# Residual stream by tokens: the second FFN products and the output projection move 512 weight columns past stationary activations

## What is computed

```python
for l in range(DEPTH):
    x = x + 0.5 * _swiglu(_rms_norm(x, ffn1_norm[l]), ffn1_w_gate[l], ffn1_w_up[l], ffn1_w_down[l])
    p = _rms_norm(x, mix_norm[l]) @ w_in[l]
    y_mla = _mla(p[..., :MLA_IN], ...)      # latent attention
    y_rwkv = _rwkv7(p[..., MLA_IN:], ...)   # recurrent mixing, in chunks of 64 tokens
    y = jnp.concatenate([_rms_norm(y_mla, out_norm_mla[l]), _rms_norm(y_rwkv, out_norm_rwkv[l])], axis=-1)
    x = x + y @ w_out[l]
    x = x + 0.5 * _swiglu(_rms_norm(x, ffn2_norm[l]), ffn2_w_gate[l], ffn2_w_up[l], ffn2_w_down[l])

def _swiglu(h, w_gate, w_up, w_down):       # 1024 -> 2816 -> 1024
    return (jax.nn.silu(h @ w_gate) * (h @ w_up)) @ w_down
```

## Time and profile before

| | |
|---|---|
| three runs | 1330.39, 1335.17, 1336.95 us (median 1335.17) |
| profiled execution, its own time | 1329.74 us |
| its span in the profile | 1328.0 us |
| mean granted TensorE clock | 0.976 of full |
| busy share of the span | TensorE 94%, weight loads 89%, VectorE 66%, ScalarE 39%, GpSimd 2% |
| read from memory | 172.57 MB, 131 GB/s over the span |

### The profile page before, as it was taken

One profiled execution on the slowest core, in us unless ns is written; L12 is line 12 of the kernel. 1 busy time (PEld: TensorE's weight loads), 2 busy tenths in 40 slices (PEclk: granted clock), 3 DMA queues, 4 the chain that ended last, 5 costly groups with the idle time before them and its releaser, 6 DMA issues.

```text
span 1328.0 us, 30142 instructions
## 1 busy us (share of the span) xinstructions
PE 1252.1 (94%) x12242; PEld 1181.2 (89%) x12242; DVE 871.3 (66%) x1498; ACT 515.8 (39%) x767; POOL 26.5 (2%) x26
## 2 busy tenths in 40 slices
PE   7999999997989999999989999999789998999998
PEld 6999999976876889999989999989668677999998
DVE  4666666687774866666666666666868558666665
ACT  3444444642121344444434444445322214344442
POOL 0000000020000000000000000000200000000000
PEclk8999999998999999999989999989999899999999
DMA  5666665531010335666546666646210103556563
GB/s 156 186 187 176 188 177 145 154 93 48 4 33 18 112 112 177 186 180 183 164 122 183 182 182 181 191 110 165 69 37 3 49 17 96 159 178 185 181 183 111
DMA packets 243396, 174.69 MB, mean 132 GB/s; under 512 B 10274, under 2 KB 228540, under 8 KB 243324
## 3 DMA queue, kind: packets, MB, share of 16 engines
q1 hardware_dynamic: 243324, 173.64, 44.6%
HBM read 172.57 MB, written 1.05 MB: 131 GB/s over the span
## 4 chain that ended last, share of the span: by engine, by line
PE 78%; DVE 16%; issue 2%; ACT 2%; DMA 2%; SPq 0%; DVEq 0%; ACTq 0%
PE bank L1247 21%; PE bank L1249 20%; PE bank L1248 20%; PE bank L1260 7%; DVE wlo L708 3%; PE bank L1271 2%; PE bank L1296 2%; ACT whi L530 1%; DVE xlo L738 1%; PE bank L1254 1%; DVE work L1072 1%; DVE root L724 1%; DVE root L725 1%; DVE work L942 1%; DMA raw<-in_ffn_w_up_dram 1%
## 5 line engine op out<-in xcount | busy, mean ns | idle before, releaser
L708 DVE TENSOR_TENSOR wlo<-raw,whi 128x1024 fp32r<-128x1024 f32 x324 | 394.8, 1221 | 261.4 <-ACT whi L530 260.5
L1247 PE MATMUL bank<-xhi,whi 128*128 128x256 f32 x1840 | 531.7, 289 | 18.7 <-DVE xlo L738 14.5
L1248 PE MATMUL bank<-xlo,whi 128*128 128x256 f32 x1840 | 524.7, 285 | 0.0
L1249 PE MATMUL bank<-xhi,wlo 128*128 128x256 f32 x1840 | 524.5, 285 | 0.0
L530 ACT ACTIVATE whi<-raw 128x1024 fp32r<-128x1024 f32 x324 | 338.7, 1049 | 307.2 <-PE bank L1249 266.3
L1247 PEld LDWEIGHTS bank<-xhi,whi 128*128 128x128 f32 x1840 | 357.7, 194 | 25.7 <-issue 11.9
L1248 PEld LDWEIGHTS bank<-xlo,whi 128*128 128x128 f32 x1840 | 357.8, 194 | 0.1
L1249 PEld LDWEIGHTS bank<-xhi,wlo 128*128 128x128 f32 x1840 | 357.3, 194 | 0.0
L1247 PE MATMUL bank<-hhi,whi 128*128 128x256 f32 x704 | 199.9, 284 | 0.8 <-DVE hlo L830 0.8
L1248 PE MATMUL bank<-hlo,whi 128*128 128x256 f32 x704 | 199.2, 283 | 0.0
L1249 PE MATMUL bank<-hhi,wlo 128*128 128x256 f32 x704 | 199.2, 283 | 0.0
(11 more groups left out here) (213 smaller groups left out, 1061.6 us busy)
## 6 DMA issues: line engine op xcount, KB each, us to landing
raw<-in_ffn_w_gate_dram SPq DMA_DIRECT2D x88, 512.0 KB, 3.9
raw<-in_ffn_w_up_dram SPq DMA_DIRECT2D x88, 512.0 KB, 3.8
raw<-in_ffn_w_down_dram SPq DMA_DIRECT2D x88, 512.0 KB, 3.5
raw<-in_w_in_dram SPq DMA_DIRECT2D x34, 512.0 KB, 4.0
raw<-in_w_out_dram SPq DMA_DIRECT2D x16, 512.0 KB, 3.3
raw<-in_w_in_dram SPq DMA_DIRECT2D x8, 256.0 KB, 3.3
raw<-in_w_q_up_dram SPq DMA_DIRECT2D x4, 384.0 KB, 3.7
work<-in_x_dram SPq DMA_DIRECT2D x1, 1024.0 KB, 6.6
```

The source lines that it names most:

```text
L708: V_.tensor_tensor(wlo[:, b.slot, 0:width], raw[:, b.slot, 0:width], whi[:, b.slot, 0:width].bitcast(F32), ALU.subtract).then_inc(lo_ready, 1)
L1247: mm(out, hi, mhi, start=start, stop=False, **kw)
L1248: mm(out, hi, mlo, start=False, stop=False, **kw)
L1249: return mm(out, lo, mhi, start=False, stop=stop, **kw)
```

## The change

x stays by tokens (the tile xtok: 128 tokens on the partitions, two of those, 1024 features along the free axis).

- The down products and the output projection swap the operands: 128 tokens of the activations are stationary, and 512 columns of the weights move. A block takes 12 matmuls of 512 columns, where it took 24 of 256. The first one of a bank starts the sum, so no bank is cleared.
- At each norm x is transposed in PSUM (turn_x, 16 transposes), after the residual is added; xhi and xlo are made from those banks. keep_clock is gone there.
- The squares are summed along the free axis by ScalarE itself (accum_out), in two instructions of 128x1024; TensorE's squares are gone.
- The row factors of the two halves of the output projection are applied by VectorE per token, in the residual (one instruction a quarter). GpSimd's additions, R's copy after rmsb and the step yn are gone.
- VectorE's splits of the second weight block (up 0, and r0 of the input projection) move from before the residual to behind the last xlo. ScalarE splits the third block before it squares.
- x is loaded and stored in four DMAs of 256 KB, without the transposes at both ends.

```diff
         def x_quarter(i):
-            return xT[:, 2 * i:2 * i + 2, :].rearrange("p t n -> p (t n)")
+            return xtok[:, i % 2, 512 * (i // 2):512 * (i // 2 + 1)]
...
-            def norm(st, phase, gain):
+            def norm(st, phase, gain, between):
                 for i in range(4):
-                    act.wait_ge(x_ready, quarter(phase, i))
+                    act.wait_ge(x_turned, turned(phase, i))
                     for t in (2 * i, 2 * i + 1):
-                        ins = nc.scalar.activation(xhi[:, t, :], xT[:, t, :], ACT.Copy, scale=col(gain, t))
+                        ins = nc.scalar.activation(xhi[:, t, :], turn_bank(phase, t), ACT.Copy, scale=col(gain, t))
                     ins.then_inc(st.sem, st.step(f"hi{i}"))
-                for i in range(4):
-                    nc.scalar.activation(xsq[:, 2 * i:2 * i + 2, :], xT[:, 2 * i:2 * i + 2, :],
-                                         ACT.Square).then_inc(st.sem, st.step(f"sq{i}"))
+                between()
+                if phase:
+                    act.wait_ge(x_ready, quarter(phase, 3))
+                for tt in range(2):
+                    ins = nc.scalar.activation(xsq[:, tt, :], xtok[:, tt, :], ACT.Square,
+                                               accum_out=stat[:, 192 + tt:193 + tt])
+                ins.then_inc(st.sem, st.step("sq"))
...
-                dve.wait_ge(stp.sem, stp.at(rnd, "ss"))
-                V_.tensor_scalar(root[:, 0, 0:2], bank[b0][:, 0:2], 1.0 / D, EPS, ALU.mult,
+                dve.wait_ge(sta.sem, sta.at(rnd, "sq"))
+                V_.tensor_scalar(root[:, 0, 0:2], stat[:, 192:194], 1.0 / D, EPS, ALU.mult,
                                  ALU.add).then_inc(st.sem, st.step("ms"))
...
-                    part = parts[:, 512 * i:512 * (i + 1)]
-                    V_.tensor_tensor(part.rearrange("p (t n) -> p t n", t=2),
...
-                        V_.tensor_tensor(x_quarter(i), x_quarter(i), part, ALU.add).then_inc(x_ready, 1)
+                    V_.scalar_tensor_tensor(x_quarter(i), bank[4 + i][:], root[:, 1, i % 2:i % 2 + 1], x_quarter(i),
+                                            ALU.mult, ALU.add).then_inc(x_ready, 1)
...
-                        rsqrt(mix_dve, l, "ym", 2)
-                        for t in range(2):
-                            ins = V_.tensor_scalar(ymla[:, t, :], ymla[:, t, :], root[:, 1, t:t + 1], None,
-                                                   ALU.mult)
-                        ins.then_inc(mix_dve.sem, mix_dve.step("yn"))
+                        rsqrt(mix_dve, l, "ym", 2, ymr[:])
...
+            def turn_x(phase):
+                for t in range(DT):
+                    if t % 4 == 0:
+                        if phase:
+                            pe.wait_ge(x_ready, quarter(phase, 1 + 2 * (t // 4)))
+                        else:
+                            pe.wait_ge(x_in[t // 4], 32)
+                    for tt in range(2):
+                        ins = turn(turn_bank(phase, t)[:, P * tt:P * (tt + 1)], xtok[:, tt, P * t:P * (t + 1)])
+                    if t % 2:
+                        ins.then_inc(x_turned, 1)
...
-                        clear(0)
                     pe.wait_ge(hlo_done, (rnd * FT + f) + 1)
-                    for t in range(DT):
-                        s = slice(P * t, P * (t + 1))
-                        ins = three(bank[t // 2][:, SEQ * (t % 2):SEQ * (t % 2 + 1)], whi[:, b.slot, s],
-                                    wlo[:, b.slot, s], hhi[:, parity, :], hlo[:, parity, :], False, last,
-                                    skip_group_check=True)
...
+                    for q in range(4):
+                        n, s = slice(P * (q % 2), P * (q % 2 + 1)), slice(512 * (q // 2), 512 * (q // 2 + 1))
+                        ins = three(bank[q][:], hhi[:, parity, n], hlo[:, parity, n], whi[:, b.slot, s],
+                                    wlo[:, b.slot, s], first, last, skip_group_check=True)
...
                 pe.wait_ge(once, ONCE)
-                keep_clock(4, 18)
+                turn_x(l * 3 + 1)
```

More of the change, by code:

```diff
@@ L835, in ffn @@
                     split(mix_block(l, MIX_BLOCKS[0]))
-                    split(mix_block(l, MIX_BLOCKS[1]))
-                else:
-                    for i in range(4):
-                        ffn_residual(l, which)(i)
             def mixing(l):
@@ L1296, in keep_clock, with column_tile @@
                     mm(bank[b][:], zeros[:, 0:P], zeros[:], start=True, stop=True)
[L1298 to L1302 removed]
             def split_ready(b):
                 pe.wait_ge(lo_ready, b.number + (RING + 1))
[L1307 removed]
+            def column_tile(b, out, wait=None):
                 for t in range(DT):
```

192 lines of the change are left out of this document (68 added, 124 removed).

## The result

The changed kernel takes **1261.4 us** (median of four runs, 1261.11 to 1262.76). The kernel before took 1333.31 us beside it (1330.39 to 1336.95). The ratio is 0.9472, 95% interval 0.9444 to 0.9500: 5.3% faster. The forecast was 1280, with a range of 1263 to 1300. The direction was right; the time lies 1.6 us under the range.

What follows compares the result with a forecast made beforehand. The prediction took TensorE, busy 94% of the span, to bound the kernel. Gains of 56.6 us, plus 6.8 and minus 8.0 for the clock, made 55.4: 1274.3 from the profiled 1329.74, so a median of 1280, range 1263 to 1300.

Steps and rivals of the forecast that it cites:

- The squares: At six norms, ScalarE sums the squares while TensorE multiplies: 3.6 us a norm, 21.6 us won.
- The fronts: From the last product before x to the stage's second block, a shorter chain at six norms: 15.4 us won.
- The clears at the first down blocks: Without four clears the first down block starts 0.1 after hlo: 0.6 us in each of four FFNs, 2.4.
- The end: At the kernel's end transposes and copies go, so the last store can follow the last residual: 3.5 us won.
- the replay: At the second norm, VectorE's chain is done at 226.4 against TensorE's 227.3: 0.9 us to spare.
- The transfer of the up block: At the third and sixth norm its wait stands ahead of xhi on ScalarE only, counted hidden by about 0.9 us.
- I count one such stretch of 3.2 us, 1.6 lost, behind each of five norms: −8.0: Half clock expected behind the new fronts, modelled on the fourth norm of before; bounds none and 18.5 us.
- clock given back: Half clock of before at the fourth norm, behind its squares and at the fifth would come back: 6.8 us won.
- the loop: In four FFN loops, a wide product takes 0.231 us against 0.240 for two narrow ones: 9.1 us won.
- the bound of 0.0133: Loop's upper bound: 0.0133 us saved a pair if that overhead is paid once per product, 13.4 us in all.
- the step from profile to median: The profiled execution of before lay 5.4 us under the median, so 1274.3 became an expected median of 1280.
- the terms for clears, shorter blocks and yn: Mixing layers: clear and shorter blocks ahead of the output projection 1.5 us a layer, yn ahead of the recurrence's copy 0.8.

Runs made afterwards that it cites:

- the added 16 products a norm: Changed kernel with 16 unused products a norm against 128 columns of ones, in the place of the squares: 1282.86 us.
- the fillers: Changed kernel with one filler ahead of the transposes at the second to sixth norm: one-column products 1387.78 us, idle time 1292.56, transposes 1296.98, zeros 1301.98.
- two kernels on both sides: Changed kernel with each wide product made as two of 256 columns: 1275.41 us; kernel before with wide products alone: 1317.92 us.
- the kernels with high halves first: Changed kernel with the xlo or wlo products last in the first two blocks of each stage: 1257.04 us; with zeros added around the first gate block's wait: 1257.92.

## Why the prediction was right or wrong

**Right, by its own steps.** The squares: 3.6 us a norm by forecast; the added 16 products a norm cost 21.5 us with no half clock behind the norms, against 21.6. The fronts: the first xlo product 2.5 us after the last down product (2.6), from the output projection's last product to the copy of R 10.0 us won at the third norm and 9.6 at the sixth (9.4). The clears at the first down blocks 0.55 each (0.6). The end 3.9 (3.5). VectorE was done 1.2 us ahead of TensorE at the second norm, where the replay had 0.9. The transfer of the up block stayed hidden.

**Wrong: the clock.** The step is "I count one such stretch of 3.2 us, 1.6 lost, behind each of five norms: −8.0". Nothing was lost, the lower bound that the text named. It took the fourth norm of before as the model, whose front had an idle 3.54 us. But by the prediction's own chain the new fronts have 16 transposes of 2 us and then half a microsecond of idle time, 0.49 in the trace. The runs show that 4.0 to 5.5 us of idle time bring half clock, and that 78 transposes in a row do not. The premise that fronts without zeros are thin fronts was false: in the fillers, transposes of 128 columns held the clock as zeros did.

The opposite cause was overlooked. The half clock at 680.5 and 881.0 stands with and behind the squares, among dense products. The prediction gave it back as "clock given back" and put the first of the two "behind its squares", without taking the squares for its cause. They are: put back, they bring it back, and in 128 columns they do not. They do not do it each time: half clock begins among the last one-column squares or just behind them at two of the six norms in the profile of before, at three in that of before with wide products, at five in that of the changed kernel with squares. So in the profile of before the squares cost their 21.6 us and some 5 more, half of 3.0 and 7.4, which stood in the sum under another name; the remaining 1.6 of its 6.8 belong to the fourth norm's front. In the changed kernel with squares they cost 36.4.

**Wrong in size: the loop.** 9.1 us by forecast, 12.2 measured, by two kernels on both sides. The 0.231 of the earlier trace rows is 0.228 in the loop, so a wide product saves 0.012 us and not 0.009, and a block 0.144 and not 0.108. The count of 21 blocks was right: 4×21×0.144 = 12.1. The 0.012 lies near the bound of 0.0133 that the text had derived and not taken.

**Wrong: the step from profile to median.** I added 5.4 us because the profiled execution of before lay that far under the median of three runs. By the four runs of the result it was 3.6. After the change the profiled execution lies on the median (1261.26 and 1261.4). The kernel before scatters over 1327.6 to 1340.1 in all its runs, the changed one over 1.7 us. With one-column squares back the runs scatter over 5.8 us, with 128 columns over 2.0. That the scatter of before came from the half clock of its squares is not shown: the kernels with high halves first have no squares and scatter over 3.8 and, with zeros, 4.6 us.

**The range.** Its low end took all clock given back, none lost and the lower bound of the wide products, 1263. What it lacked is the first mixing block: from the copy of R to the last product of the output projection 3.8 us are won, where the terms for clears, shorter blocks and yn have 2.3; in the second block it is 1.8. The first block of before takes 2.1 us longer than its second, and 1.9 of them have come up within 87 us behind R; the two blocks of the changed kernel are alike. Windows over the half clock there, in the kernel before and in the changed one:

```profile
294.30:311.40 17.10, 11.11 (x32) 6.72 (x32) 14.61 (x29) 2.39 (x5) 6.04 (x5) 0.60 0.21 65
956.50:963.30 6.80, 4.12 (x13) 2.41 (x13) 6.20 (x14) 0.36 (x1) 1.63 (x1) 0.50 0.25 78
```

```profile
279.00:293.00 14.00, 10.49 (x26) 4.83 (x25) 12.68 (x25) 2.39 (x5) 7.85 (x7) 0.51 0.13 37
900.20:913.80 13.60, 10.72 (x26) 5.03 (x27) 12.48 (x24) 2.22 (x5) 7.96 (x7) 0.50 0.11 39
```

The first block of before has more half clock than its second, but the changed kernel has as much in both, and 85 us behind R both are as far as the second of before was. So the cause of this part stays open.

## What to carry to other kernels

Count what an engine does in a front before calling it thin: here half clock came behind idle times of 4.0 to 5.5 us and with products of one column, and 62 transposes or 34 products with zeros in a row held full clock. A sum over partitions by one-column products can cost more than its own time, in half clock on the dense products behind it (15.0 us over six norms); where it must stay on TensorE, 128 columns took the same time in place. And order the products of a stage by when their operands come, high halves first: that took another 0.8 us from each norm.

## What was not expected of the hardware

- One-column fp32 products take TensorE's granted clock to 0.50 although the engine shows as busy without a gap: of 24 us of them in a row, some 20 ran at half clock.
- A product of 512 columns with its own weight load starts every 0.228 us, one of 256 every 0.120. The Trainium skill, "TensorE: Matmul & The Clock Gate", Back-to-back issue gap, gives N/2.4 + 2.5 ns for the isolated gap, by which a pair differs by 2.5 ns; in the loops of two experiments here it is 12.
- fp32 products against one column and against 128 columns of ones took the same 1.25 us for four and the triple behind them.
